# A hybrid mixer and mixture-of-experts layer on one core: when outputs are scaled, when GpSimd copies its columns, and what is loaded first

## The reference, cut to what matters

```
proj = rms_norm(h, norm_mix_g) @ w_in              # h = [meta_tokens; x]
...
h = h + mixed @ w_out
t = rms_norm(h, norm_ffn_g)                        # groups, then the 2 best experts of one group
for e in range(16):
    he = silu(t @ w_gate[e]) * (t @ w_up[e])       # 1024 -> 512
    y  = y + gates[:, e:e+1] * (he @ w_down[e])    # 512 -> 1024
out = rms_norm(h + y, final_norm_g)[:, 16:]
```

## Time and profile before

| | us |
|---|---|
| median of three runs | 1161.17 |
| profiled execution | 1167.15 |
| its span | 1165.4 |
| TensorE busy in it | 1063.2 (91%) |
| VectorE, ScalarE, GpSimd busy | 831.6, 642.6, 464.7 |
| experts, from the first gathered rows turned to the last down chunk | 699.5 to 1137.3 |

### The profile page before, as it was taken

One profiled execution on the slowest core, in us unless ns is written; L12 is line 12 of the kernel. 1 busy time (PEld: TensorE's weight loads), 2 busy tenths in 40 slices (PEclk: granted clock), 3 DMA queues, 4 the chain that ended last, 5 costly groups with the idle time before them and its releaser, 6 DMA issues. The chain is left out here.

```text
span 1165.4 us, 21292 instructions
## 1 busy us (share of the span) xinstructions
PE 1063.2 (91%) x7144; PEld 892.6 (77%) x7144; DVE 831.6 (71%) x1214; ACT 642.6 (55%) x1013; POOL 464.7 (40%) x301
## 2 busy tenths in 40 slices
PE   4899989999986989999999929999999999989997
PEld 4898989889986846676666718878888888878875
DVE  4797856647248566455555378888888988888996
ACT  5522111165633358454444327878888888878874
POOL 1122211223100126111112213777877887868960
PEclk9999989999997899999999969999999999999999
DMA  7125434342024460001111494997899999753345
GB/s 273 49 81 65 115 96 123 106 122 88 21 60 89 155 235 17 1 38 54 55 56 73 150 372 171 380 368 273 253 386 366 371 332 366 229 181 61 119 101 243
DMA packets 89494, 194.99 MB, mean 167 GB/s; under 512 B 9264, under 2 KB 32048, under 8 KB 88768
## 3 DMA queue, kind: packets, MB, share of 16 engines
q1 hardware_dynamic: 82800, 169.93, 42.3%
q0 software_dynamic: 6624, 24.12, 8.6%
HBM read 157.70 MB, written 31.51 MB: 162 GB/s over the span
## 5 line engine op out<-in xcount | busy, mean ns | idle before, releaser
L2329 PE MATMUL ps<-weights_higher,split 128*128 128x512 f32 x1136 | 310.5, 395 | 0.0
L493 PE MATMUL ps<-xsplit,wsplit 128*128 128x384 f32 (+2 forms) x1440 | 242.0, 326 | 2.6 <-POOL wsplit L265 2.6
L2329 PEld LDWEIGHTS ps<-weights_higher,split 128*128 128x128 f32 x1136 | 210.5, 189 | 42.0 <-ACT split L2393 0.2
L493 PEld LDWEIGHTS ps<-xsplit,wsplit 128*128 128x128 f32 x1440 | 228.7, 191 | 3.8 <-POOL wsplit L265 3.0
L2388 ACT CAST weights_higher<-gate_up 128x1024 fp32r (+1 forms) x192 | 199.9, 1054 | 48.4 <-PE ps L2329 45.3
L2469 DVE TENSOR_TENSOR weights_lower<-gate_up,weights_higher 128x1024 fp32r<-128x1024 f32 x144 | 182.4, 1317 | 11.8 <-ACT weights_higher L2388 11.3
L2329 PE MATMUL ps<-weights_lower,split 128*128 128x512 f32 x568 | 176.7, 392 | 6.2 <-DVE weights_lower L2469 6.1
L265 POOL TENSOR_TENSOR wsplit<-mem,wsplit 128x1024 fp32r<-128x1024 f32 x22 | 57.8, 2628 | 248.6 <-ACT wsplit L348 248.6
L2268 POOL TENSOR_TENSOR weights_lower<-gate_up,weights_higher 128x1024 fp32r<-128x1024 f32 x48 | 122.0, 2541 | 67.6 <-ACT weights_higher L2388 66.2
L2329 PEld LDWEIGHTS ps<-weights_lower,split 128*128 128x128 f32 x568 | 106.3, 188 | 31.9 <-DVE weights_lower L2469 8.8
L2469 DVE TENSOR_TENSOR weights_lower<-weights,weights_higher 128x1024 fp32r<-128x1024 f32 x72 | 111.3, 1594 | 20.1 <-ACT weights_higher L2388 20.0
(11 more groups left out here) (442 smaller groups left out, 1786.8 us busy)
## 6 DMA issues: line engine op xcount, KB each, us to landing
weights<-in_w_down SPq DMA_DIRECT2D x16, 2048.0 KB, 17.5
gate_up<-in_w_gate SPq DMA_DIRECT2D x30, 1024.0 KB
gate_up<-in_w_up SPq DMA_DIRECT2D x30, 1024.0 KB
mem<-in_w_in SPq DMA_DIRECT2D x22, 512.0 KB, 4.2
mem<-in_x SPq DMA_DIRECT2D x10, 512.0 KB, 3.5
mem<-in_w_out SPq DMA_DIRECT2D x1, 4096.0 KB, 15.5
h_d<-mem SPq DMA_DIRECT2D x8, 512.0 KB, 2.6
xn_d<-mem SPq DMA_DIRECT2D x8, 512.0 KB, 2.6
```

The lines of the kernel that those rows point to most:

```text
L493: mm = nc.tensor.matmul(ps[:, n % 6, 0:hi - lo], w[slot_of(h)][:, k % 4, P * m:P * m + P], x[:, k, lo:hi], start=(k == 0 and p_ == 0), sto ...
L2329: mm = nc.tensor.matmul(ps[:, bank + h, :], x, w[place % RING][:, 512 * h:512 * h + 512], start=(k == 0 and p_ == 0), stop=(k == n - 1 and ...
```

## The change

Three places of the program are moved; what is computed stays the same.

- **Outputs.** VectorE's `outputs_of(b-1)` moves from behind place 2 to behind place 6 (`KD - 2`). `hidden_lower` stays.
- **Columns.** GpSimd's `columns(b)` moves from behind place 3 to behind place 11 (`KD + RING - 1`), its last subtraction of the block; in the last pair it stays behind place 3.
- **Launch.** SyncE loads meta tokens, norm weights, first 128 tokens, identity alone (64 KB), the next 128 tokens, the two first weight halves, the other tokens in pairs, and the rest of the constants (440 KB) after that. VectorE no longer waits for all of these at its start: for the first tile it waits for norm weights and identity, right before the product with the weights. TensorE waits for the rest of the constants only behind the first six products. ScalarE does a square root ahead of the first square, copies tile 1 ahead of both weight halves, and copies tile 2 ahead of the square of tile 3; VectorE subtracts tile 2 ahead of the norm of tile 3.

```diff
         def sp_project(sp):
-            for t in range(9):
-                if t < 3:
-                    src = a["meta_tokens"] if t == 0 else a["x"][P * (t - 1):P * t, :]
-                    sp.dma_start(XN[0:rows(t), t, :], src).then_inc(x_loaded[t], 16)
...
-                if t == 0:
-                    sp.dma_start(GAIN, a["norm_mix_g"].to_broadcast([P, D])).then_inc(params_loaded, 16)
-                    for lo, hi in ((0, C_TRI), (C_TRI, C_COS)):
-                        sp.dma_start(con[:, lo:hi], a["consts"][:, lo:hi]).then_inc(params_loaded, 16)
-                if t in (2, 3):
-                    sp_half(sp, t - 2)
+            sp.dma_start(XN[0:META, 0, :], a["meta_tokens"]).then_inc(x_loaded[0], 16)
+            sp.dma_start(GAIN, a["norm_mix_g"].to_broadcast([P, D])).then_inc(params_loaded, 16)
+            sp.dma_start(XN[:, 1, :], a["x"][0:P, :]).then_inc(x_loaded[1], 16)
+            sp.dma_start(ident, a["consts"][:, C_ID:C_ID + P]).then_inc(params_loaded, 16)
+            sp.dma_start(XN[:, 2, :], a["x"][P:2 * P, :]).then_inc(x_loaded[2], 16)
+            for h in range(2):
+                sp_half(sp, h)
+            for t in range(3, 9, 2):
+                sp.dma_start(XN[:, t:t + 2, :], a["x"][P * (t - 1):P * (t + 1), :].rearrange("(t p) d -> p t d", p=P)).then_inc(x_loaded[XG_OF[t]], 16)
+            sp.wait_ge(params_loaded, 32)
+            sp.dma_start(con[:, C_ID + P:C_COS], a["consts"][:, C_ID + P:C_COS]).then_inc(params_loaded, 16)
...
         def act_project(act, link):
...
             for t in range(10):
+                if t == 3:
+                    copies(2)
                 if t < 9:
...
+                    if t == 0:
+                        nc.scalar.activation(SD[0:R, 0:1], XN[0:R, 0, 0:1], ACT.Sqrt, scale=0.0)
...
+                if t >= 1 and t != 3:
+                    copies(t - 1)
+                for h in {2: (0, 1), 7: (2,), 8: (3,)}.get(t, ()):
+                    act_higher(act, h)
...
         def dve_norm(dve, link, t):
...
+            if t == 0:
+                dve.wait_ge(params_loaded, 32)
...
         def dve_project(dve, link):
-            dve.wait_ge(params_loaded, 48)
             for t in range(10):
+                if t == 3:
+                    dve_lower(dve, 2)
...
         def pe_project(pe):
-            pe.wait_ge(params_loaded, 48)
+            pe.wait_ge(params_loaded, 32)
...
         def pool_experts(pool):
...
-                    if place == RING - 1 and not (par and last):
-                        if not first:
-                            pool.wait_ge(ye_stored, 16 * b - 16)
-                        columns(b, par, False)
                     if place == 2 * RING - 1 and (par or not first):
...
+                    if place == (RING - 1 if last else KD + RING - 1) and not (par and last):
+                        if not first:
+                            pool.wait_ge(ye_stored, 16 * b - 16)
+                        columns(b, par, False)
...
         def dve_experts(dve, link):
...
                     elif place == (RING if first and not par else RING - 1):
-                        if par or not first:
-                            outputs_of(b - 1, 1 - par, first)
                         hidden_lower(b, HH, HLO)
+                    elif place == KD - 2 and (par or not first):
+                        outputs_of(b - 1, 1 - par, first)
```

More of the change, by code:

```diff
@@ L281, in sp_project @@
         def sp_project(sp):
-            for t in range(9):
-                if t < 3:
-                    src = a["meta_tokens"] if t == 0 else a["x"][P * (t - 1):P * t, :]
-                    sp.dma_start(XN[0:rows(t), t, :], src).then_inc(x_loaded[t], 16)
-                elif t % 2:
-                    sp.dma_start(XN[:, t:t + 2, :], a["x"][P * (t - 1):P * (t + 1), :].rearrange("(t p) d -> p t d", p=P)).then_inc(x_loaded[XG_OF[t]], 16)
-                if t == 0:
-                    sp.dma_start(GAIN, a["norm_mix_g"].to_broadcast([P, D])).then_inc(params_loaded, 16)
-                    for lo, hi in ((0, C_TRI), (C_TRI, C_COS)):
-                        sp.dma_start(con[:, lo:hi], a["consts"][:, lo:hi]).then_inc(params_loaded, 16)
-                if t in (2, 3):
-                    sp_half(sp, t - 2)
+            sp.dma_start(XN[0:META, 0, :], a["meta_tokens"]).then_inc(x_loaded[0], 16)
[9 more added lines that the diff above has]
+            sp.dma_start(con[:, C_ID + P:C_COS], a["consts"][:, C_ID + P:C_COS]).then_inc(params_loaded, 16)
             for h in (2, 3):
@@ L300, in sp_project @@
             sp.dma_start(con[:, C_COS:C_END], a["consts"][:, C_COS:C_END]).then_inc(x_loaded[0], 16)
+            sp.wait_ge(params_loaded, 48)
             sp.dma_start(GN, a["hgrn_norm_g"].to_broadcast([P, 64])).then_inc(params_loaded, 16)
@@ L350, in act_project, with copies @@
         def act_project(act, link):
+            def copies(t):
+                lo, hi = cols(t)
+                for j in range(2):
+                    act.wait_ge(xt_ready, 2 * t + j + 1)
+                    nc.scalar.copy(XHI[:, 4 * j:4 * j + 4, lo:hi],
+                                   ps[:, 6 + j, 0:4 * (hi - lo)].rearrange("p (k t) -> p k t", k=4)).then_inc(xhi_ready, 1)
             for t in range(10):
+                if t == 3:
+                    copies(2)
                 if t < 9:
@@ L450, in dve_project @@
         def dve_project(dve, link):
-            dve.wait_ge(params_loaded, 48)
             for t in range(10):
+                if t == 3:
+                    dve_lower(dve, 2)
                 if t < 9:
                     dve_norm(dve, link, t)
-                if t >= 1:
+                if t >= 1 and t != 3:
                     dve_lower(dve, t - 1)
+            dve.wait_ge(params_loaded, 48)
             dve.wait_ge(x_loaded[0], 32)
@@ L514, in pe_project @@
                 pe_first_products(pe, n).then_inc(proj_done, 1)
+            pe.wait_ge(params_loaded, 48)
             for g in range(2, 2 * NS):
```

## The result

The changed kernel takes 1189.3 us (median of four runs, 1182.5 to 1190.5) where the kernel before takes 1160.9 (1160.1 to 1166.0): ratio 1.021, interval 1.018 to 1.024. It is slower, as forecast, but by 28 us instead of 9, and outside the range. The profiled executions took 1190.53 and 1167.15 us, 23.4 apart; the one before was 6.2 us above its median and the other 1.2, which is the difference to 28. The work of the experts, from their first product to their last, went from 701.27 to 1137.23 before (435.96) and goes from 704.45 to 1160.57 now (456.12): 20.2 us are lost there and 3.2 ahead of it.

A forecast was written before the change was run, and what follows sets the result against it. TensorE was taken to set the experts' pace at 17.7 us per ordinary block. Launch -2.7, outputs -5.9 and columns +18 summed to +9.4 us, so the median 1161.2 became 1170.6 us, range 1152 to 1177.

The forecast's parts named there:

- -5.9 forecast: VectorE's outputs behind place 6: no scatter landing is waited for, so two long blocks lose 5.9 us; bounds -6.5 and -4.
- -2.7 forecast: Launch: earlier tokens and weight-half copies end the first product sooner, -2.7 us, bounds -4 and -0.4.
- 13.9 to 18.6: Launch: GpSimd's two subtractions run back to back, 2.36 us each, from 13.9 to 18.6; the second ended at 19.22 before.
- 22.5: Launch: forecast time in us at which TensorE's first product ends, 2.9 us before the earlier 25.38.
- +18 forecast: Columns behind place 11: slow copies delay GpSimd's place 3, costing 12 blocks 1.5 us each; bounds 9 and 22.
- the race for place 4: GpSimd's place 3 against VectorE's place 4: TensorE loses 1.7 us if VectorE starts first, 0.8 if GpSimd; 1.5 taken.
- In how many blocks?: Columns: step counting blocks with a loss from 22 index copies, 13 slow and nine quick; 12 blocks taken.
- there three more copies of about 0.13 fit, and nothing is lost: Columns: in nine even blocks where ScalarE starts late, the copies run before VectorE's first subtraction and cost nothing.
- The loss does not heal: Columns: ScalarE, VectorE and GpSimd follow TensorE's chunk count, so the next block finds the same order; 1.5 us per block stays.
- The columns cost nothing: First rival: column copies fall into gaps, total loss below 2.8 us, time 1152.6 us; chance 0.27.
- GpSimd wins the race: Second rival: GpSimd starts before VectorE's place 4 or more copies slip, columns cost 11 us, time 1164; chance 0.20.
- The third: Third rival: after the outputs' move the scatter's landing is still waited for, 5.9 us stay, time 1176.5; chance 0.08.

The follow-up runs named there:

- the part alone: The kernel before with only the outputs moved behind place 6: 1158.1 us, ratio 0.996; for the launch, with only the launch changed: 1161.4 us, ratio 0.998.
- first pair alone: The changed kernel with columns behind place 11 in the first pair of blocks only, behind place 3 in all others: 1160.3 us, ratio 0.999 to the kernel before.

## Why the prediction failed, point by point

**Outputs: right.** -5.9 forecast, -5.7 measured by the part alone; no landing is waited for.

**Launch: right direction, size off.** -2.7 forecast, -1.3 in the changed kernel's trace and -2.0 in the trace of the part alone. The mis-sized term is GpSimd's two subtractions, "13.9 to 18.6": the copy of a weight half that the first one waits for was put at 13.8 and takes 1.04, so the sum's own numbers give 14.84 to 19.56, and 14.78 to 19.47 was measured. That is most of the 1.0 us by which the first product ends behind 22.5. The landing of the first tokens was off too, 6.4 taken and 7.5 measured (the norm weights land 4.9 us after their issue and not 3.9 "in both orders"), but the copies started at 13.65 all the same, and it can have moved only the first pass, from 16.0 to 16.84, which then waited for GpSimd. The rest was lost behind the first product: TensorE's eight transposes at 23.32 took 1.61 us where those at 25.19 took 1.06 before.

**Columns: the sign right, the block count, the price and the reason wrong.** +18 forecast (12 blocks of 1.5), +26.5 measured (429.66 to 456.12 us; some 20 blocks of 1.28 and one of 18.15). In the changed kernel the slow copies, their cause and their end with VectorE's third subtraction were as forecast, and the rule of the Trainium skill (SBUF — State Buffer, "SBUF: two separate sides") held: each slow copy waits for one whole subtraction (1.20 us beside VectorE's 1.22). GpSimd won the race for place 4 (0.8 us forecast for that case).

The step that failed is "In how many blocks?", with "there three more copies of about 0.13 fit, and nothing is lost" for the nine even blocks and 1.5 us for twelve others. I read the slack of the kernel before, block by block, as if each block would start on time; but the copies are in GpSimd's round, and with them the whole round takes longer than TensorE's 17.72. Then every block starts as late as that round makes it, VectorE stands beside place 11 and the copies in even blocks too, and the quick copies are gone. The runs with copies in every second block show it. Copies at the starts of the odd blocks alone, where the forecast has its losses, cost 2.8 us over the experts: nine of these eleven blocks take 17.7 to 17.8 us where 19.2 was forecast, and only the first, 18.92 to 19.12 us in the four runs that have copies there, is near its price. Copies at the starts of the even blocks alone, where it has none, cost 3.5. Both together cost 26.5 (432.42, 433.18 and 456.12 against 429.66). So the +18 isn't a smaller part of the 26.5: in a loop on time most of the priced blocks lose nothing, and that the sum pointed the right way is partly luck. "The loss does not heal" was right by its words for copies in every block and wrong by its reason: the next block finds a later order, not the same one; and it does heal where the next block has no copies (first pair alone).

**Ahead of the experts** the changed kernel lost 3.2 us in its profiled execution although its launch gained 1.3. Windows of the changed kernel with a granted clock (the third column from the end) below 1:

```profile
95.00:101.00 6.00, 4.88 (x23) 4.13 (x24) 5.86 (x6) 0.57 (x1) 0.00 (x0) 0.72 0.78 89
256.00:260.00 4.00, 3.88 (x17) 3.92 (x18) 3.97 (x3) 1.87 (x3) 0.30 (x1) 0.57 0.42 149
434.00:438.00 4.00, 4.00 (x18) 2.17 (x17) 0.61 (x1) 0.98 (x2) 2.35 (x1) 0.57 0.81 194
```

Stretches of 3.4 us at half clock lie in these three (6.00 x 0.28 x 2, 4.00 x 0.43 x 2), and none in the execution before at those times. Their sum over the span was 84.3 us in the changed kernel, 67.0 before, and 57.3 to 82.4 in the other profiled executions (the clock's records summed), whose experts start between 695.8 and 705.0 us without regard to the launch that they have. Ahead of the experts alone it was 75.8 us against 58.2. Over all 16 profiled executions the experts start some 0.3 us later for each us of this sum (correlation 0.88), so 17.6 us more of it go with about 5 us, enough for the 3.2 and the launch's 1.3. This is a fit over executions, not an experiment, and why a given execution has more of these stretches stays open. They are large enough to hide a gain of 2 us at the launch.

**The rivals.** "The columns cost nothing" is out. "GpSimd wins the race" was right for the race and wrong for the time, since it left the block count. The third, that the scatter's landing is still waited for, is out: no such wait is left. The chain that ended last agrees with the reading: 11% of the span on GpSimd now, 0% before.

```profile
PE 19%; POOL 11%; issue 7%; POOLq 2%; ACT 2%; DVE 2%; DMA 1%; ACTq 0%; DVEq 0%
```

## What to carry to other kernels

Work put into an engine's queue between two steps that each wait for the other's chain has to be priced on the whole round of the loop, not on the slack of one block: add up the engine's way from a step to itself one iteration later, with the waits that depend on it, and compare it with the pace of the bound engine. In these runs every iteration paid where the sum with the delays of a late start was above that pace (19.0 against 17.72), and a delay healed where it was below, without copies in the next block. The small GpSimd operations cost nothing where GpSimd has to wait anyway, here behind place 3 or behind place 7, though three and two of the copies are slow there. Their number counts only up to what stands beside them on VectorE: behind place 11 four, three, two and one copies, with the index copy behind each, gave experts of 452.75, 456.12, 450.92 and 432.32 us, and behind place 3 leaving one out was worth nothing.

## What the hardware showed that was not expected

- A row of one-column copies on GpSimd (0.18 us each alone) costs as many of VectorE's subtractions as stand beside it, three at most here, at 1.17 to 1.24 us each: two, three or four copies with the index copy behind them gave 8.52, 8.63 and 8.74 us from place 11 to place 3.
- VectorE's places 4 to 6 stand in the records from 834.20, 0.63 us before GpSimd's subtraction at 834.83, yet that one took 2.40 us undelayed and the three took 6.38, the first of them 4.12, to 1.1 us behind GpSimd's end: an instruction's recorded start on VectorE is not the time from which it holds GpSimd up.
- The products at the launch take 0.25 us each (3.99 for 16) and at 24.68 0.136 (3.26 for 24), while the granted clock reads 1.00 in the window of both:

```profile
6.00:26.00 20.00, 13.54 (x66) 12.40 (x67) 12.06 (x21) 11.25 (x23) 4.69 (x2) 1.00 0.94 349
```

The trace's clock records begin only at 24.48 us (25.23 in the kernel before), and where there is none, the column reads 1.00. In all 16 traces the median from one product's start to the next is 0.227 us ahead of the first record and 0.125 or 0.126 behind it. So the prediction's reading, the first product on the lower clock and the second on the higher, holds, and the first record (21.29 to 25.77 us in these traces) tells when the rate changed. In the changed kernel it lies among the eight transposes at 23.32, which is why they took 1.61 us.
